# Order and engines around the last two products of a two-block transformer kernel: three held slabs, an earlier split, residual additions moved

## What is computed

```python
def second_block(x, ...):
    h = x
    ...                                   # norm, w_in, convolution, attention
    mixed = jnp.concatenate([conv_out, attn_out], axis=-1)
    y = jnp.einsum("bsc,cd->bsd", mixed, w_out[l])
    h = h + _rmsnorm(y, g_post_mix[l])
    f_in = _rmsnorm(h, g_pre_ffn[l])
    gt = jnp.einsum("bsd,df->bsf", f_in, w_gate[l])
    up = jnp.einsum("bsd,df->bsf", f_in, w_up[l])
    f = jnp.einsum("bsf,fd->bsd", jax.nn.silu(gt) * up, w_down[l])
    h = h + _rmsnorm(f, g_post_ffn[l])
    return h
```

## Time and profile before

| | |
|---|---|
| median of 3 runs | 1910.54 us (1905.37 to 1910.64) |
| the profiled execution's own time | 1910.52 us |
| its span in the profile | 1908.7 us |
| mean granted clock | 0.978 |
| PE busy | 1822.8 us, 96% of the span |
| DVE busy | 958.7 us, 50% |
| ACT busy | 752.3 us, 39% |
| POOL busy | 152.1 us, 8% |
| HBM | 82 GB/s over the span |

### The profile page before, as it was taken

One profiled execution on the slowest core, in us unless ns is written; L12 is line 12 of the kernel. 1 busy time (PEld: TensorE's weight loads), 2 busy tenths in 40 slices (PEclk: granted clock), 3 DMA queues, 4 the chain that ended last, 5 costly groups with the idle time before them and its releaser, 6 DMA issues.

```text
span 1908.7 us, 21603 instructions
## 1 busy us (share of the span) xinstructions
PE 1822.8 (96%) x8477; PEld 1488.6 (78%) x8477; DVE 958.7 (50%) x1690; ACT 752.3 (39%) x1474; POOL 152.1 (8%) x181
## 2 busy tenths in 40 slices
PE   7899999999999999999999999998998889999997
PEld 5777888888887777777888888786777678888885
DVE  5555443444344666765443434489954444233345
ACT  6333242323233655654232323423765343232232
POOL 0011010101010021001010101010020100000000
PEclk9999999999999999999999999999998899999999
DMA  6222223233322211112323333232100232333321
GB/s 232 68 66 67 88 88 100 89 100 98 100 96 81 73 56 56 38 49 79 100 90 99 99 100 93 76 86 77 45 11 1 77 111 89 99 100 100 97 91 55
DMA packets 195748, 158.37 MB, mean 83 GB/s; under 512 B 5248, under 2 KB 161152, under 8 KB 195648
## 3 DMA queue, kind: packets, MB, share of 16 engines
q1 hardware_dynamic: 194240, 154.16, 26.3%
q0 software_dynamic: 400, 1.25, 0.3%
q10 hardware_dynamic: 1008, 1.59, 0.2%
HBM read 154.88 MB, written 2.10 MB: 82 GB/s over the span
## 4 chain that ended last, share of the span: by engine, by line
PE 83%; DVE 12%; ACT 3%; issue 1%; DMA 0%; SPq 0%; ACTq 0%; DVEq 0%
PE ps L758 27%; PE ps L759 26%; PE ps L760 26%; DVE sb L2255 3%; DVE sb L1860 2%; PE ps L810 1%; PE ps L1189 1%; DVE sb L2381 1%; DVE sb L1874 1%; ACT sb L1395 0%; DVE sb L2020 0%; PE ps L1077 0%; PE ps L1083 0%; ACT sb L1387 0%; ACT sb L1408 0%
## 5 line engine op out<-in xcount | busy, mean ns | idle before, releaser
L758 PE MATMUL ps<-sb,sb 128*128 128x512 f32 (+4 forms) x2547 | 994.2, 393 | 24.2 <-DVE sb L1860 7.6
L759 PE MATMUL ps<-sb,sb 128*128 128x512 f32 (+4 forms) x2547 | 971.0, 383 | 0.0
L760 PE MATMUL ps<-sb,sb 128*128 128x512 f32 (+4 forms) x2547 | 970.7, 383 | 0.0
L758 PEld LDWEIGHTS ps<-sb,sb 128*128 128x128 f32 (+1 forms) x2547 | 481.6, 190 | 134.5 <-issue 19.0
L760 PEld LDWEIGHTS ps<-sb,sb 128*128 128x128 f32 (+1 forms) x2547 | 481.4, 190 | 94.0
L759 PEld LDWEIGHTS ps<-sb,sb 128*128 128x128 f32 (+1 forms) x2547 | 482.2, 190 | 86.1
L1860 DVE TENSOR_TENSOR sb<-sb,sb 128x512 fp32r<-128x512 f32 x532 | 357.5, 712 | 353.9 <-ACT sb L1387 353.0
L1387 ACT ACTIVATE sb<-sb 128x512 fp32r<-128x512 f32 x532 | 305.2, 622 | 444.4 <-PE ps L760 444.4
L2059 DVE TENSOR_TENSOR sb<-sb,sb 128x512 fp32r<-128x512 f32 x64 | 68.0, 1063 | 177.0 <-ACT sb L1529 177.0
L1539 ACT ACTIVATE sb<-ps 128x512 f32<-128x512 f32 x64 | 38.4, 599 | 208.3 <-PE ps L760 208.3
L656 POOL TENSOR_TENSOR sb<-sb 128x512 f32<-128x512 f32 x64 | 66.9, 1045 | 608.1 <-ACT sb L1539 608.1
(11 more groups left out here) (202 smaller groups left out, 1046.0 us busy)
## 6 DMA issues: line engine op xcount, KB each, us to landing
sb<-in_w_up SPq DMA_DIRECT2D x86, 512.0 KB, 3.9
sb<-in_w_down SPq DMA_DIRECT2D x86, 512.0 KB, 3.9
sb<-in_w_gate SPq DMA_DIRECT2D x22, 512.0 KB, 3.7
sb<-in_a_w_in SPq DMA_DIRECT2D x20, 512.0 KB, 3.7
sb<-in_w_in SPq DMA_DIRECT2D x20, 512.0 KB, 3.7
sb<-in_w_o SPq DMA_DIRECT2D x16, 512.0 KB, 3.9
sb<-in_w_mem_kv SPq DMA_DIRECT2D x8, 512.0 KB, 7.3
sb<-in_w_out SPq DMA_DIRECT2D x8, 512.0 KB, 3.9
```

What stands on the lines that cost most here:

```text
L758: mm(ps, lh, rh, start=start, stop=False, **k)
L759: mm(ps, lh, rl, start=False, stop=False, **k)
L760: return mm(ps, ll, rh, start=False, stop=stop, **k)
```

## The change

- `last_strips` takes a list of (n, j) and holds as many slabs as the list has. Both products pass their last three: (1,2), (0,3), (1,3) for w_out, (1,1), (0,2), (1,2) for the last group of w_down. `next_slab` for each stands in front of its first strip (tile 0), not all of them ahead of the first strip. The order of the slabs in the list is as before.
- ACT and DVE split gt 0 (`weights(SL["gt", 0] + 1)`) ahead of the squares of X and of the turns; u2 0 stays where both were.
- The residual additions of h = 1 of tiles 0 to 2 go from POOL to DVE in both places; `post_pool` is gone, and `post_dve` counts two per tile. In the first place DVE's order for a tile is now: `post_b`, both multiplications, both additions, then `post_a` of the next tile. Before, it was `post_b`, multiplication 0, `post_a` of the next tile, addition 0, multiplication 1.
- Waits on X and the stores follow the new counts. The load of `g_post_ffn` waits for the eight multiplications only.

```diff
-    for n, j in [(n, j) for n in range(2) for j in range(3)] + [(0, 3), (1, 3)]:
+    OUT = [(0, 0), (0, 1), (0, 2), (1, 0), (1, 1), (1, 2), (0, 3), (1, 3)]
+    for n, j in OUT:
...
-            return (S("post_pool"), t + 1) if t < 3 else (S("post_dve"), 5)
+            return S("post_dve"), 2 * t + 2
...
-            q.wait_ge(S("post_dve"), 5 + t + 1)
+            q.wait_ge(S("post_dve"), 8 + 2 * t + 1)
...
-        def post(c):
-            for t in range(3):
-                q.wait_ge(S("post_v"), 8 * c + 2 * t + 2)
-                TTT(X[:, t, 512:1024], TF[:, t, 512:1024], X[:, t, 512:1024], ALU.add).then_inc(S("post_pool"), 1)
-
-        post(0)
-        q.wait_ge(S("post_dve"), 5)
         q.wait_ge(S("post_v"), 8)
         e.dma_start(GP[:, :], ins["g_post_ffn_2"].broadcast_to([128, D])).then_inc(S("gp"), 16)
-        post(1)
...
-        def last_strips(step, done):
-
-            w = [next_slab(), next_slab()]
+        def last_strips(order, step, done):
+
+            w = []
             for t in range(4):
-                for n in range(2):
-                    m = step(w[n], n, t)
-                    m.then_inc(S("w_used") if t == 3 else S(done), 1)
+                for i, (n, j) in enumerate(order):
+                    if t == 0:
+                        w.append(next_slab())
+                    m = step(w[i], j, n, t)
+                    if t == 3:
+                        m.then_inc(S("w_used"), 1)
+                    elif i > 0:
+                        m.then_inc(S(done), 1)
...
-        for n, j in ((0, 1), (0, 2), (1, 0), (1, 1), (1, 2)):
+        for n, j in OUT[1:5]:
...
-        last_strips(lambda w, n, t: out_strip(w, 3, n, t), "o_tile")
+        last_strips(OUT[5:], out_strip, "o_tile")
...
-            for n, j in ((1, 0), (1, 1), (1, 2), (1, 3)) if g < 2 else ((0, 0), (0, 1), (1, 0), (1, 1)):
+            for n, j in ((1, 0), (1, 1), (1, 2), (1, 3)) if g < 2 else DN[:3]:
...
-        last_strips(lambda w, n, t: down_strip(w, 2, n, t), "d_tile")
+        last_strips(DN[3:], down_strip, "d_tile")
...
             rsqrt(("post", 0, t), 1)
+        weights(SL["gt", 0] + 1)
         for t in range(2):
             square(X, "pre_ffn", t)
...
-            if t < 3:
-                q.wait_ge(S("post_pool"), 3 + t + 1)
-            else:
-                q.wait_ge(S("post_dve"), 10)
+            q.wait_ge(S("post_dve"), 8 + 2 * t + 2)
...
-            if c == 1:
-                q.wait_ge(S("post_pool"), min(t + 1, 3))
...
             post_b(0, t)
-            post_mul(0, t, 0)
+            for h in range(2):
+                post_mul(0, t, h)
+            for h in range(2):
+                post_add(0, t, h)
             if t < 3:
                 post_a(0, t + 1)
-            post_add(0, t, 0)
-            post_mul(0, t, 1)
-        post_add(0, 3, 1)
+        weights(SL["gt", 0] + 1)
         for k in range(4):
             turn("pre_ffn", Ah, Al, "pre_ffn", k)
...
             post_mul(1, t, 1)
+            post_add(1, t, 1)
             if t < 2:
                 last_sum(t + 2)
-        post_add(1, 3, 1)
```

More of the change, by code:

```diff
@@ L1391, in square @@
             q.wait_ge(*x_ready(job, t))
-            if job == "pre_ffn":
-                q.wait_ge(S("post_dve"), min(t + 1 + (t == 3), 5))
             q.wait_ge(S("sq"), SQN[job] + t)
```

## The result

The changed kernel takes 1896.62 us at the median (1893.97 to 1897.85, 6 runs), the one before 1910.47 beside it (1905.32 to 1915.05, 6 runs). The ratio is 0.9932, with a 95% interval of 0.9914 to 0.995, so 13.0 us less (9.6 to 16.4). The profiled execution took 1897.68 us, its span is 1895.9: 12.8 less than before.

What follows compares the result with a forecast made beforehand. PE was taken as the bound (83%, DVE 12%), with gains only where it stands still: 9.1 us in the first place plus 3.1 at the end, 12.2 off 1910.52, gives 1898.3 us. The range was 1894.5 to 1903.5.

Steps and rivals of the forecast that it cites:

- The tiles' pace, hold, margin: Last products: three held slabs make tiles end 4.08 us apart instead of 2.72; third slab's split has 0.6 us margin.
- DVE's 3.96 us a tile: After the output product: DVE's cost per tile, 1.44 + 1.32 + 1.20 us, just below PE's 4.08, so tile 3 isn't queued.
- part 2: Residual additions moved from POOL to DVE; with the hold, 4.3 us in the first place; alone at the end, 0.3.
- The stalls beside POOL: DVE instructions beside POOL's additions: three stalls of about 1.1 us in the first place, 2.5 us in all at the end, go.
- the lower end of the bound: Load of `g_post_ffn` before the last additions: cost bounded between 0 and 0.57 us, taken as 0.
- The early split: After the output product: gt 0 split ahead of the squares lets PE begin k = 4's turn at 1523.33 instead of 1532.71.
- From k = 4's turn to the spread: First gated tile: from k = 4's turn at 1523.33 to the spread at 1532.3, against 1541.37 before.
- two paths that meet here: Ahead of the spread: the root on DVE ends at 1532.2, PE's products at 1532.0.
- the rival of a low clock through all of gt 0: PE's clock stays low through gt 0: 14.2 us from k = 4's turn, gain 3.9 instead of 9.1, 1903.5 us; chance 0.15.
- The end: Kernel's end: tile 0's chain starts 2.72 us earlier, moved additions net 0.3; gain 3.0 to 3.1 us.
- The rivals that would have ended slower or without effect: Clock low far into the gated product, 1918 us, chance 0.03; hold not effective, tile 3 queued, 1903.5 us, chance 0.08.

Runs made afterwards that it cites:

- u_pool: The kernel before with the hold and the early split, additions of h = 1 still on POOL in the old order; 1899.79 us, ratio 0.9948 to the kernel before.
- f_fused: The changed kernel with the gain multiplied in while the root is computed, scaling joined to the residual addition, tile 1's end sum behind tile 0's additions; 1893.39 us, ratio 0.9916.
- f_root: f_fused with ACT's squares in idle gaps, u2 0's split behind the turns, the root's first DVE step ahead of that split's low part; 1890.64 us, ratio 0.9904.
- after_again: The changed kernel once more, unaltered, run beside the later variants on the same chip; 1897.59 us, ratio 0.9936 to the kernel before.

## Why the prediction was right, point by point

- **The tiles' pace, hold, margin.** Second squares were forecast from 1504.2 on at 4.08 us; they came at 1503.76 and 1507.84, 0.45 us earlier because the output product as a whole was. The third split was ready at 1501.70, and counting ten strips back from the end of the product it was needed at about 1502.2: a margin of 0.5 us, where 0.6 was forecast. PE shows no wait there, and 2.20 us when it is asked for ahead (2.1 forecast).
- **DVE's 3.96 us a tile.** Shown with two slabs held: 3.95 and 3.96. This was the thin step, 0.12 us below PE's pace, and it held. With the additions on POOL DVE keeps up as well (4.08 us between sums in u_pool); what part 2 gains is the shorter chain behind tile 3's sum, forecast 1521.23 - 1517.18 = 4.05 and measured 4.04. X was ready 1520.77 - 1515.58 = 5.19 us behind the last matmul; forecast 1521.23 - 1516.03 = 5.20.
- **The stalls beside POOL.** They went, and came back with 1.26 us in u_pool. In the first place only the one in tile 3's chain costs time once three slabs are held, 1.10 of the 2.02 us; the rest is DVE's new order. The Trainium skill, SBUF — State Buffer, section "Who interferes with whom", describes such a lock between a GpSimd instruction that reads SBUF and a VectorE instruction with two SBUF inputs; the end at the same moment (1515.5) agrees. The section gives that rule; that the additions should go to DVE is the prediction's own conclusion. The load of the gain beside two additions cost nothing (1.28 us with it and without), the lower end of the bound. The Trainium skill infers as much in the same section of SBUF — State Buffer, and this one load agrees.
- **The early split.** The turn of k = 4 was forecast 1523.33 - 1516.03 = 7.30 behind the last matmul; it was 7.23. The split alone is worth 5.0. The prediction booked 9.1 for the place, 4.3 of it for hold and additions together; by P these are 16.68 - 7.23 = 9.45, of which hold and additions 4.31 to 4.49.
- **From k = 4's turn to the spread.** Forecast 8.97, measured 8.77, but 9.93 in a second profile of the same kernel. The prediction had two paths that meet here. The root on DVE was forecast 1532.2 - 1516.03 = 16.2 behind the last matmul and came at 15.94; it set the spread. PE's products were forecast at 16.0 and ended at about 15.8, by two terms that were off in opposite directions: the clock cost less than in the old trace, from which the 5.92 us were taken over (the turn of k = 4 to the fourth product's end took 5.40), and the four bare products took 3.14 instead of 2.74, since PE stood for a low part of DVE's ahead of them. That part of the fit is luck. In the second profile three pairs took 2.17, 2.13 and 1.75 us and PE set the spread; that is about a fifth of the way from the forecast to the rival of a low clock through all of gt 0 (14.2). The rival's size was never reached in any run (10.13 at most, in f_fused), but its mechanism is real. In that profile it cost 1.2 us. A full clock would by the timeline give nothing back in the changed kernel, because the root comes at 15.94 and behind the first turns it doesn't wait for PE; no run tests this.
- **The end.** Forecast 3.0 to 3.1, measured 3.05, of which the hold 2.68 to 2.72 and the additions 0.33 to 0.36 (0.3 forecast).
- **The rivals that would have ended slower or without effect** didn't occur: PE's clock was at 1.00 over the whole gated product (353.90 us against 353.84 before), and the hold moved A by 3.85.
- **The total.** 12.2 forecast, 12.4 in the two places, 12.8 between the two spans, 13.0 (9.6 to 16.4) by the ratio.

## What to carry to other kernels

When an engine serves tiles that another one finishes, compare the two paces before paying for an earlier finish: here DVE's 3.96 us a tile just fit below PE's 4.08. And look at parts together: the moved additions were worth 0.6 us while DVE lagged behind PE, since their work delayed the last tile's sum, and 2.0 to 2.2 once three slabs were held and DVE had room for them. Ask for a resource at its first use, not at the head of the group (4.4 us here). And behind the last value of a chain leave as few instructions as possible: multiplying by the gain while the root was being computed, with one partial sum moved behind an addition, took two more us off the end.

The version that came out of it, f_root, runs at 0.9904 (0.9886 to 0.9922) of the kernel before, against 0.9936 (0.9919 to 0.9954) for the changed one on the same chip. The two intervals overlap slightly, though the slowest of f_root's 4 runs (1890.69) is below the fastest of the changed kernel's 6 beside it (1893.35); in the stages P is 1.05 us and B 2.03 us shorter.

## What the runs showed of the hardware

**The same code up to the output product ends at times up to 5.6 us apart.** Its last matmul starts at 1510.64 us in after_again and at 1516.20 in f_fused, with 1515.58 in the first profile of the changed kernel; what PE does before the held strips is the same in all. Two stretches of the changed kernel's two profiles, the first one's row above, the second's below:

```profile
1400.00:1450.00 50.00, 49.98 (x255) 40.84 (x255) 21.30 (x28) 31.98 (x44) 6.06 (x4) 0.93 0.00 1
```

```profile
1400.00:1450.00 50.00, 47.88 (x259) 39.09 (x258) 22.55 (x33) 34.94 (x50) 5.04 (x2) 1.00 0.00 1
```

In the first, low stretches of the clock (two, with a mean of 0.66 over 1418 to 1423 and over 1435 to 1440) fell into 50 us in which PE was saturated, in the second none did. They began while PE was busy without a break, so idle time isn't the only thing a low clock follows. An estimate of what the low clock cost, from rows of 1 us up to 1515 (PE's busy time in each, times one minus the clock in it, added up), gives 24.4 us in the first profile and 21.0 in the second, so 3.4 of the 4.9 us between these two. What makes up the rest isn't shown. The differing phases of the clock are likely why medians of one kernel differ by some us from one set of runs to the next, and why effects below 3 us were read from stages.
